# Latent norms moved between the first products, and the last feed-forward pair moved in front of the last full group, in a two-block transformer kernel

## The reference, cut to what matters

```python
def rms_norm(x, gain=None):
    xf = x.astype(jnp.float32)
    y = (xf * lax.rsqrt(jnp.mean(xf * xf, axis=-1, keepdims=True) + EPS)).astype(x.dtype)
    return y if gain is None else y * gain
def mla_q(cq, g_q, w_uq, cos, sin, rope):
    ...
    q = (rms_norm(cq, g_q) @ w_uq).reshape(B, T, MLA_HEADS, MLA_NOPE + MLA_ROPE)
    ...
def mla_kv(ckv, kr, g_kv, w_uk, w_uv, cos, sin, rope):
    ...
    ckv = rms_norm(ckv, g_kv)
    k_nope = (ckv @ w_uk).reshape(B, T, MLA_HEADS, MLA_NOPE)
    v = (ckv @ w_uv).reshape(B, T, MLA_HEADS, MLA_V)
    ...
def multiscale_pool(p, w_pool, s_pool):
    ...
        outs.append(d @ w_pool[g])
    return jnp.concatenate(outs, axis=-1) * s_pool
def conv_ffn(h, w_up, conv_w, conv_b, w_down):
    a = h @ w_up
    g, u = a[..., :D_FF], a[..., D_FF:]
    ...
    return (jax.nn.silu(acc) * u) @ w_down
```

## Time and profile before

| | us |
|---|---|
| median of three runs | 2871.48 (2870.13 to 2874.97) |
| the profiled execution | 2874.07 |
| its span | 2872.3 |
| TensorE busy | 2712.1 (94%) |
| VectorE busy | 1590.7 (55%) |
| ScalarE busy | 1001.6 (35%) |
| GpSimd busy | 100.4 (3%) |
| mean granted TensorE clock | 0.967 of full |

### The profile page before, as it was taken

The page is one execution under the profiler, slowest core; times in us unless marked ns, Lnnn a source line. Parts: engine busy times, 40 slices in busy tenths (PEclk is TensorE's granted clock), DMA queues, the critical chain, the costliest instruction groups (busy, mean ns, idle before and its releaser), DMA issues. The chain is left out here.

```text
span 2872.3 us, 36109 instructions
## 1 busy us (share of the span) xinstructions
PE 2712.1 (94%) x14552; PEld 2210.9 (77%) x14552; DVE 1590.7 (55%) x2467; ACT 1001.6 (35%) x1562; POOL 100.4 (3%) x123
## 2 busy tenths in 40 slices
PE   7979899999999989998999999999989999999997
PEld 4758787888888867777888877788867777777775
DVE  6478835333333356776544455466654666656566
ACT  3145533222221233554333323322333434333343
POOL 0100000000000000000000000000000000000000
PEclk9979999999999989999999999999989999999998
DMA  6520013333333311011322223222222222222221
GB/s 230 164 88 30 24 44 103 104 117 105 106 116 107 103 45 52 23 37 57 112 92 92 95 81 125 88 88 87 85 73 74 82 83 83 72 77 86 87 76 44
DMA packets 67243, 246.97 MB, mean 86 GB/s; under 512 B 7504, under 2 KB 7888, under 8 KB 66384
## 3 DMA queue, kind: packets, MB, share of 16 engines
q1 hardware_dynamic: 52144, 188.55, 19.4%
q0 software_dynamic: 14800, 55.65, 6.3%
q10 hardware_dynamic: 144, 0.52, 0.1%
HBM read 242.45 MB, written 2.24 MB: 85 GB/s over the span
## 5 line engine op out<-in xcount | busy, mean ns | idle before, releaser
L2147 DVE TENSOR_TENSOR WL<-RAW,WH 128x1024 fp32r<-128x1024 f32 x331 | 405.2, 1225 | 642.8 <-ACT WH L1575 642.5
L766 PE MATMUL PS<-HM,WH 128*128 128x512 f32 x1752 | 701.8, 401 | 16.6 <-DVE HM L2154 7.2
L767 PE MATMUL PS<-HM,WH 128*128 128x512 f32 x1752 | 696.2, 397 | 0.0
L768 PE MATMUL PS<-HM,WL 128*128 128x512 f32 x1752 | 695.2, 397 | 0.0
L1575 ACT ACTIVATE WH<-RAW 128x1024 fp32r<-128x1024 f32 x331 | 349.6, 1057 | 798.3 <-PE PS L768 789.7
L766 PEld LDWEIGHTS PS<-HM,WH 128*128 128x128 f32 x1752 | 331.3, 189 | 89.6 <-issue 26.4
L768 PEld LDWEIGHTS PS<-HM,WL 128*128 128x128 f32 x1752 | 330.6, 189 | 79.2
L767 PEld LDWEIGHTS PS<-HM,WH 128*128 128x128 f32 x1752 | 331.5, 189 | 55.9
L766 PE MATMUL PS<-GM,WH 128*128 128x512 f32 x468 | 186.3, 398 | 4.3 <-DVE GM L2154 3.7
L767 PE MATMUL PS<-GM,WH 128*128 128x512 f32 x468 | 187.0, 399 | 0.0
L768 PE MATMUL PS<-GM,WL 128*128 128x512 f32 x468 | 186.5, 398 | 0.0
(11 more groups left out here) (398 smaller groups left out, 4614.8 us busy)
## 6 DMA issues: line engine op xcount, KB each, us to landing
RAW<-in_tiles SPq DMA_DIRECT2D x333, 512.0 KB, 3.3
MRAW<-in_mods POOLq DMA_DIRECT2D x80, 512.0 KB, 5.1
TB<-bias_rows POOLq DMA_DIRECT2D x16, 576.0 KB, 6.3
FIRST<-in_mods SPq DMA_DIRECT2D x8, 1024.0 KB, 17.6
X_M<-in_x SPq DMA_DIRECT2D x1, 2048.0 KB, 12.6
VN_GB<-in_gm_rows POOLq DMA_DIRECT2D x2, 1024.0 KB, 5.9
out_x<-X_M SPq DMA_DIRECT2D x8, 256.0 KB, 2.1
X_C<-in_ctx SPq DMA_DIRECT2D x1, 1024.0 KB, 14.4
```

What stands on the lines that cost most here:

```text
L766: pe.matmul(out_, wh, xh, start=first, stop=False, skip_group_check=True)
L767: pe.matmul(out_, wh, xl, start=False, stop=False, skip_group_check=True)
L768: return pe.matmul(out_, wl, xh, start=False, stop=last, skip_group_check=True)
L2147: dve.tensor_tensor(WL[:, s.mod(2), :], RAW[:, s.mod(2), :], f32(WH[:, s.mod(2), :]), ALU.subtract).then_inc(tile_split[s.mod(2)], 1)
```

## The change

Latent norms. `cq` and `ckv` join `COMPACT`; the `stats` form goes, with its two big roots and reciprocals. ScalarE squares a `LAT` tile (768 wide, one instruction) in the loop over the ten products. TensorE makes the one-column sums of cq's first two tiles behind products 5 and 6 and of the third in the middle of product 7 (`amid`, after step 3 of 8), the main spread of cq behind product 7, its context spread in the middle of product 8, the sums of ckv behind product 8 and in the middle of product 9, and both spreads of ckv behind product 9. VectorE scales `LAT` in place; the high and low parts are made behind product 9 (768 wide). The pool products keep their order but use other banks (`pool_unit`) and wait for other reads; their low parts on VectorE now stand behind the low parts of cq, two of them behind those of ckv. Modulation rows 16 to 19 and their turn move: 16 before the fourth pool product, 17 behind the queries, 18 behind the keys, 19 behind the values, the turn behind the first two scores.

Feed-forward. In both layers pair 21 now stands in front of down group 4, which is followed by group 5. Units, tiles and load order follow; the last modulation pair moves from group 4 into pair 21.

```diff
+        def downs_ahead(f):
+            return min(max(0, f - 1) // GROUP, FFN_GROUPS - 2)
         def ffn_pair(layer, f):
-            downs = max(0, f - 1) // GROUP
+            downs = downs_ahead(f)
...
         def ffn_down(layer, g):
             count = min(GROUP, FC - GROUP * g)
-            f = min(GROUP * g + GROUP, FC - 1)
+            f = GROUP * g + GROUP if g < FFN_GROUPS - 2 else FC - 1
             s, u = ffn_pair(layer, f)
-            return At((s + 2).start), At((u + 2).start), count
+            last = g == FFN_GROUPS - 1
+            return At((s + 2).start + (GROUP if last else 0)), At((u + 2).start + (KC if last else 0)), count
...
+            def latent_sums(name, j):
+                _, c0 = NORM[name]
+                pe.wait_ge(sq_ready, c0 + j + 1)
+                for b in range(BLOCKS):
+                    mm = pe.matmul(norm_sums(name)[:, b:b + 1], SQ[:, (c0 + j) % 2, b * P:(b + 1) * P], ONES[:, 0:1],
+                                   start=(j == 0 and b == 0), stop=(j == (2 if name == "cq" else 1)), skip_group_check=True)
+                mm.then_inc(sq_used, 1)
...
+            def cq_context_spread():
+                pe.wait_ge(norm_scaled, SPLITS["cq"] + 1)
+                pe.matmul(rb_ctx("cq"), ONES[:, :], RB[:, 0:TC], start=True, stop=True, skip_group_check=True).then_inc(rb_spread, 1)
+
+            amid = {7: lambda: latent_sums("cq", 2), 8: cq_context_spread, 9: lambda: latent_sums("ckv", 1)}
             for n in range(2, 10):
-                gemm(s + n, u + n, HM, HC)
+                gemm(s + n, u + n, HM, HC, amid=amid[n] if n >= 7 else None)
                 mod_rows(6 + n)
+                if n in (5, 6):
+                    latent_sums("cq", n - 5)
+                elif n == 7:
+                    pe.wait_ge(diag_ready, SPREAD["cq_ctx"])
+                    pe.matmul(rb_main("cq"), ONES[:, :], RB[:, TC:TA], start=True, stop=True, skip_group_check=True).then_inc(rb_spread, 1)
+                elif n == 8:
+                    pe.wait_ge(norm_scaled, SPLITS["ckv"])
+                    latent_sums("ckv", 0)
+            pe.wait_ge(acc_read, UNIT["in"] + 9)
+            norm_spread("ckv", True)
...
             for g in range(4):
-                u = At(UNIT["pool_w"]) + g
-                pe.wait_ge(acc_read, u.times() if g == 0 else (u - 2).times())
+                u = pool_unit(g)
+                if g == 2:
+                    pe.wait_ge(norm_scaled, SPLITS["ckv"] + 1)
+                else:
+                    pe.wait_ge(acc_read, UNIT["in"] + (8, 10, 0, 11)[g])
...
-            mod_rows(16)
-            pe.wait_ge(acc_read, UNIT["pool_w"] + 3)
-            stats("cq", 3, True)
-            mod_rows(17)
-            stats("ckv", 2, True)
-            mod_rows(18)
-            pe.wait_ge(acc_read, UNIT["mix_out"])
+                if g == 2:
+                    mod_rows(16)
...
             pe.wait_ge(norm_ready, SPLITS["ckv"])
+            pe.wait_ge(acc_read, UNIT["pool_w"] + 2)
             main_queries(0)
-            mod_rows(19)
+            mod_rows(17)
             pe.wait_ge(norm_ready, SPLITS["ffn0"])
             context_products(0)
+            pe.wait_ge(acc_read, UNIT["mix_out"])
             main_keys(0)
-            mod_turn(2)
+            mod_rows(18)
             value_products(0, 0)
             value_products(0, 1)
+            mod_rows(19)
             scores(0)
             scores(1)
+            mod_turn(2)
...
                 for f in range(FC):
                     pair(f)
-                    if f and f % GROUP == 0:
+                    if f and f % GROUP == 0 and f // GROUP < FFN_GROUPS - 1:
                         down(f // GROUP - 1)
+                down(FFN_GROUPS - 2)
                 down(FFN_GROUPS - 1)
```

134 lines of the change are left out of this document (70 added, 64 removed).

## The result

The changed kernel takes 2847.91 us (median of 4 runs, 2843.62 to 2850.66), against 2870.81 for the kernel before beside it. The ratio is 0.9918, with a 95% interval of 0.9906 to 0.9931. Forecast were 2842 and a range of 2837 to 2852: the direction is right, the median lies 5.9 us above the value and inside the range. A later group of runs of the same kernel has its median at 2853.2, just outside, so the place inside the range is in part luck.

What follows compares the result with a forecast made beforehand. TensorE, busy 94% of the span, was taken to bound the kernel. Gains of 17.0 us up to the latent scores and 5.8 and 6.6 at the feed-forward ends sum to 29.4, from median 2871.48 to 2842; range 2837 to 2852.

Steps and rivals of the forecast that it cites:

- the loop: Latent attention from the scores on: same work in the same order, so the shift should last to the end.

## What to carry to other kernels

Moving a norm's short chain under products that are bound by TensorE pays in full as long as each input is ready when its instruction comes up, as it was here; count TensorE's added time one for one. Where a kernel has pauses of 2 to 4 us on TensorE, any change ahead of them that shifts them in time can win or lose a few microseconds at each. Carry a term of plus or minus 5 us for the unchanged rest (my estimate, from 4.9 gained in the loop and 5.3 lost at the hole), and read a gain at the place where it arises before reading it at the end. Compare the distance between the same two instructions in several traces before blaming the change.

## What the hardware showed that I hadn't expected

- TensorE's clock can fall while the engine is busy 10.00 of 10 us: behind twelve one-column float32 matmuls in a row (24 instructions, 2.8 us), 512 columns take 0.63 us for some 3 us, at three places of five. Behind six (1.4 us) it stayed at 0.39 at all five.
- Behind one and the same hole of 3.08 us the first matmuls read 0.39 to 0.40, 0.63 at once, or 0.63 after the fourth. Three traces in which the hole comes within 0.4 us of the same time from the start show all three.
- Two executions of one program can start their first product 1.9 us apart (38.09 and 39.96 us), with a granted clock of 0.92 and 0.50 from 30 to 36 us.
- Two traces of the kernel before hold a distance of 0.3 to 0.5 us over the whole span. Two of the changed kernel part by 3.9 us in one place (the second is 1.9 ahead at the tenth product and 2.0 behind at the first row maximum), with the clock at 1.00 in one and 0.51 in the other; from there on it stays 1.3 to 2.8 behind.
